# Hybrid diffusion trunk: RMSNorm by token-major statistics, with squares taken tile by tile and the high parts first

## The reference

```python
def _rmsnorm(x, g):
    xf = x.astype(jnp.float32)
    y = xf * lax.rsqrt(jnp.mean(xf * xf, axis=-1, keepdims=True) + NORM_EPS)
    return (y * g.astype(jnp.float32)).astype(x.dtype)
...
        h = _rmsnorm(x, W["norms"][l, 0]) * (1 + sc1) + sh1
        x = x + 0.5 * g1 * _swiglu(h, W["ffn_w1"][l, 0], W["ffn_w3"][l, 0], W["ffn_w2"][l, 0])
        h = _rmsnorm(x, W["norms"][l, 1]) * (1 + sc2) + sh2
        ...
        x = x + g2 * m.astype(x.dtype)
        h = _rmsnorm(x, W["norms"][l, 2]) * (1 + sc3) + sh3
        x = x + 0.5 * g3 * _swiglu(h, W["ffn_w1"][l, 1], W["ffn_w3"][l, 1], W["ffn_w2"][l, 1])
    return _rmsnorm(x, W["final_norm"]), (ak, av, bs, ck, cv)
```

## Time and profile before

| | us |
|---|---|
| timed runs, median of 3 | 3680.97 (3680.93 to 3685.23) |
| profiled execution, its own time | 3675.11 |
| its span | 3673.3 |
| PE busy | 3193.1 (87%) |
| DVE busy | 1676.1 (46%) |
| ACT busy | 981.8 (27%) |

### The profile page before, as it was taken

How to read it: one execution, slowest core, us unless ns; L and a number is a source line. 1 busy time by engine, 2 the same in 40 slices (tenths; PEclk the granted TensorE clock), 3 DMA queues, 4 the chain that set the end, 5 groups by cost and what they waited for, 6 DMA issues and landing times.

```text
span 3673.3 us, 61594 instructions
## 1 busy us (share of the span) xinstructions
PE 3193.1 (87%) x26174; PEld 2984.0 (81%) x26174; DVE 1676.1 (46%) x2575; ACT 981.8 (27%) x1724; POOL 0.2 (0%) x4
## 2 busy tenths in 40 slices
PE   7799998987688878899998999998975555899998
PEld 7799998975576667899998999998952224899997
DVE  2554545544445543554545454544135554422323
ACT  1212123213333322212123212123234343222222
POOL 0000000000000000000000000000000000000000
PEclk6899999986678888999999999999977667999999
DMA  6243433200000002244433444442200002222221
GB/s 213 69 120 109 124 111 92 75 14 0 16 5 4 5 4 75 83 113 120 126 95 100 109 121 116 113 121 62 69 8 6 4 6 60 58 69 80 70 79 52
DMA packets 393646, 264.16 MB, mean 72 GB/s; under 512 B 11627, under 2 KB 375430, under 8 KB 393350
## 3 DMA queue, kind: packets, MB, share of 16 engines
q1 hardware_dynamic: 393478, 261.71, 25.2%
HBM read 257.61 MB, written 4.06 MB: 71 GB/s over the span
## 4 chain that ended last, share of the span: by engine, by line
PE 82%; DVE 11%; ACT 3%; issue 2%; DMA 1%; SPq 0%; DVEq 0%; ACTq 0%
PE pair L2386 62%; PE pair L2372 2%; PE pair L1699 1%; PE pair L2352 1%; PE pair L2395 1%; DVE big L2206 1%; PE pair L829 1%; PE pair L812 1%; PE pair L1694 1%; PE pair L421 1%; DVE w_lo_as_f L1808 1%; PE pair L396 1%; DVE work L2200 1%; PE pair L1685 1%; PE pair L823 1%
## 5 line engine op out<-in xcount | busy, mean ns | idle before, releaser
L2386 PE MATMUL pair<-h_hi,w_hi 128*128 128x320 f32 x3792 | 874.7, 312 | 114.5 <-DVE h_lo L2215 68.1
L2386 PE MATMUL pair<-h_lo,w_hi 128*128 128x320 f32 x3792 | 872.6, 312 | 0.0
L2386 PE MATMUL pair<-h_hi,w_lo 128*128 128x320 f32 x3792 | 871.0, 311 | 0.0
L2386 PEld LDWEIGHTS pair<-h_hi,w_hi 128*128 128x128 f32 x3792 | 641.3, 190 | 118.3 <-issue 118.3
L2386 PEld LDWEIGHTS pair<-h_lo,w_hi 128*128 128x128 f32 x3792 | 642.3, 190 | 0.0
L2386 PEld LDWEIGHTS pair<-h_hi,w_lo 128*128 128x128 f32 x3792 | 641.7, 190 | 0.0
L2386 PE MATMUL pair<-big_as_f32r,w_hi 128*128 128x320 f32 x2816 | 540.6, 315 | 4.5 <-DVE w_lo L2105 4.5
L1995 ACT ACTIVATE w_hi<-raw 128x1024 fp32r<-128x1024 f32 x333 | 341.3, 1051 | 637.6 <-PE pair L2386 336.4
L2105 DVE TENSOR_TENSOR w_lo<-raw,w_hi 128x1024 fp32r<-128x1024 f32 x333 | 398.0, 1217 | 167.4 <-ACT w_hi L1995 166.7
L2386 PEld LDWEIGHTS pair<-big_as_f32r,w_hi 128*128 128x128 f32 x2816 | 453.5, 193 | 5.3 <-DVE w_lo L2105 5.3
L2250 DVE TENSOR_TENSOR work<-work,pair 128x640 f32<-128x640 f32 x88 | 72.3, 821 | 639.4 <-PE pair L2386 639.4
(11 more groups left out here) (346 smaller groups left out, 2868.0 us busy)
## 6 DMA issues: line engine op xcount, KB each, us to landing
raw<-ffn_w SPq DMA_DIRECT2D x272, 512.0 KB, 5.1
work<-mod_w SPq DMA_DIRECT2D x136, 512.0 KB, 3.8
raw<-w_in_c SPq DMA_DIRECT2D x24, 512.0 KB, 3.7
raw<-w_in_ab SPq DMA_DIRECT2D x21, 512.0 KB, 4.0
w_hi_as_f<-mod_w SPq DMA_DIRECT2D x8, 512.0 KB, 4.6
raw<-w_out_ab SPq DMA_DIRECT2D x8, 512.0 KB, 5.7
raw<-w_out_c SPq DMA_DIRECT2D x8, 512.0 KB, 5.1
h_hi_as_f<-x_sample SPq DMA_DIRECT2D x1, 2048.0 KB
```

The source lines that it names most:

```text
L2386: ins = nc.tensor.matmul(ps[:, c, 0:HALF], w, v[:, k, c * HALF:(c + 1) * HALF], start=(k == 0 and w is hi and v is xh), stop=(k == kts - 1 ...
```

## The change

For norms 1 to 6 the squares no longer stand in the norm. In the stage ahead of it ACT squares tile j right after DVE has updated it, into two small buffers in turn (the first tile straight into the sum), and DVE adds the tiles 1 to 6 into `sq_acc`; the last square stays apart. Norm 0 still squares its eight tiles first.

The mean is formed with tokens on the partitions: the squares are the weights, 64 tokens at a time, and one column of 1/1024 is the moving operand, so 20 calls of one column for two parts (80 for norm 0's eight). Root and reciprocal work on `rt5`, 128 tokens by 5, and five matmuls spread it over the partitions into the pair that DVE then reads while scaling. That pair is `norm_pair(k)`, `pp[(norm_at[k] + 2) % 4]`, no longer the one of the next stage's first slab. ACT's load of the root's table is put at the start of the stage ahead.

After a norm PE takes the first two slabs together (`two_slabs`): all products with `h_hi` of both, tile by tile as `n_hi` comes, then those with `h_lo`.

```diff
+        sq_acc = work[:, 5376:6016]
+        sq_t = (work[:, 4096:4736], work[:, 4736:5376])
+        rt5 = work[:, 6016:6021]
...
+        def norm_pair(k):
+            return pp[(norm_at[k] + 2) % 4]
...
-                for t in range(DT):
-                    if k:
-                        act.wait_ge(pair_free, norm_at[k] + RING - DT + t + 1)
-                    nc.scalar.activation(norm_t[:, t, :], x[:, t, :], ACT.Square).then_inc(n_sq, 1)
+                if k == 0:
+                    for t in range(DT):
+                        nc.scalar.activation(norm_t[:, t, :], x[:, t, :], ACT.Square).then_inc(n_sq, 1)
                 act.wait_ge(n_sum, k + 1)
-                nc.scalar.activation(halves(rt_t), pp[norm_at[k] % 4][:, :, 0:HALF], ACT.Sqrt, bias=eps[:, 0:1]).then_inc(n_root, 1)
+                nc.scalar.activation(rt5, norm_pair(k)[:, 0, 0:NCH], ACT.Sqrt, bias=eps[:, 0:1]).then_inc(n_root, 1)
...
                 elif kind in ("down", "out"):
+                    if before_norm(i):
+                        nc.scalar.preload_act_table(ACT.Sqrt)
                     for j in range(cnt):
                         if j + 2 < cnt or ahead:
                             split_hi(0, n0 + j + 2)
+                        if before_norm(i):
+                            act.wait_ge(pair_free, n0 + j + 1 + RING)
+                            if j > 2:
+                                act.wait_ge(n_acc, (DT - 2) * (norm_after(i) - 1) + j - 2)
+                            nc.scalar.activation(sq_t[j % 2] if j else sq_acc, x[:, j, :], ACT.Square).then_inc(n_sq, 1)
...
-                nc.vector.reciprocal(rt_t, rt_t).then_inc(n_recip, 1)
-                dve.wait_ge(n_recip, k + 1)
+                nc.vector.reciprocal(rt5, rt5).then_inc(n_recip, 1)
+                dve.wait_ge(n_spread, k + 1)
...
-                                                             in1=rt_t[:, a:b], op0=ALU.mult, op1=ALU.mult)
+                                                             in1=norm_pair(k)[:, g, 0:b - a], op0=ALU.mult, op1=ALU.mult)
...
+                        if before_norm(i) and j >= 2:
+                            k = norm_after(i)
+                            dve.wait_ge(n_sq, DT * k + j)
+                            if j > 2:
+                                dve.wait_ge(n_acc, (DT - 2) * (k - 1) + j - 2)
+                            nc.vector.tensor_tensor(sq_acc, sq_acc, sq_t[(j - 1) % 2], ALU.add).then_inc(n_acc, 1)
...
-                pair = pp[norm_at[k] % 4]
+                pair = norm_pair(k)
                 if k == 0:
                     pe.wait_ge(m_taken, COLUMNWISE * DT // 4 + 2)
+                    pe.wait_ge(mod_fin, 2)
+                    parts = [norm_t[:, t, :] for t in range(DT)]
                 else:
-                    pe.wait_ge(pair_free, norm_at[k] + 1)
-                for t in range(DT):
-                    pe.wait_ge(n_sq, DT * k + t + 1)
-                    for c in range(2):
-                        ins = nc.tensor.matmul(pair[:, c, 0:HALF], mean_d, norm_t[:, t, c * HALF:(c + 1) * HALF],
-                                               start=(t == 0), stop=(t == DT - 1))
+                    pe.wait_ge(pair_free, norm_at[k] + 3)
+                    pe.wait_ge(n_acc, (DT - 2) * k)
+                    parts = [sq_acc, sq_t[(DT - 1) % 2]]
+                for t, part in enumerate(parts):
+                    if k == 0 or t:
+                        pe.wait_ge(n_sq, DT * k + (t + 1 if k == 0 else DT))
+                    for j in range(NCH):
+                        for h in range(2):
+                            ins = nc.tensor.matmul(pair[h * HD:(h + 1) * HD, 0, j:j + 1],
+                                                   part[:, j * P + h * HD:j * P + (h + 1) * HD], mean_d[:, 0:1],
+                                                   start=(t == 0 and j == 0), stop=(t == len(parts) - 1), skip_group_check=True)
                 ins.then_inc(n_sum, 1)
+                pe.wait_ge(n_recip, k + 1)
+                for j in range(NCH):
+                    ins = nc.tensor.matmul(pair[:, j // 4, j % 4 * P:(j % 4 + 1) * P], rt5[:, j:j + 1].to_broadcast([P, P]), ident,
+                                           start=True, stop=True)
+                ins.then_inc(n_spread, 1)
...
+            def two_slabs(n0, kk):
+
+                for j in (n0, n0 + 1):
+                    pe.wait_ge(lo_full, j + 1 + RING)
+                    pe.wait_ge(pair_free, j + 1)
+                for k in range(DT):
+                    pe.wait_ge(n_hi, DT * kk + k + 1)
+                    for j in (n0, n0 + 1):
+                        for w in (w_hi, w_lo):
+                            for c in range(2):
+                                nc.tensor.matmul(pp[j % 4][:, c, 0:HALF], w[:, j % RING, k, :], h_hi[:, k, c * HALF:(c + 1) * HALF],
+                                                 start=(k == 0 and w is w_hi), stop=False)
+                for j in (n0, n0 + 1):
+                    for k in range(DT):
+                        if j == n0:
+                            pe.wait_ge(n_lo, DT * kk + k + 1)
+                        for c in range(2):
+                            ins = nc.tensor.matmul(pp[j % 4][:, c, 0:HALF], w_hi[:, j % RING, k, :], h_lo[:, k, c * HALF:(c + 1) * HALF],
+                                                   start=False, stop=(k == DT - 1))
+                    ins.then_inc(slab_used, 1)
...
+                    if key in norm_before:
+                        two_slabs(n0, norm_before[key])
+                        slab(0, n0 + 2, kts, k0, xh, xl, None)
+                        slab(0, n0 + 3, kts, k0, xh, xl, None)
```

More of the change, by code:

```diff
@@ L178, in build @@
         prod_t = work[:, 4736:5376].rearrange("p (a b) -> p a b", a=2)
-        rt_t = work[:, 5376:6016]
+        sq_acc = work[:, 5376:6016]
+        sq_t = (work[:, 4096:4736], work[:, 4736:5376])
+        rt5 = work[:, 6016:6021]
         def col(i, n=1):
@@ L220, in build @@
         n_sq, n_sum, n_root, n_recip, n_scaled, n_hi, n_lo = NM
+        n_acc, n_spread = sem("norm_acc"), sem("norm_spread")
         stages = []
@@ L265, in halves2, with before_norm, norm_after @@
             return ap[:, t, :].rearrange("p (a b) -> p a b", a=2)
+        def before_norm(i):
+            return i + 1 == len(stages) or stages[i + 1][:4] in norm_before
+        def norm_after(i):
+            return NORMS - 1 if i + 1 == len(stages) else norm_before[stages[i + 1][:4]]
+        def norm_pair(k):
+            return pp[(norm_at[k] + 2) % 4]
         def LOOKAHEAD(i):
@@ L2420, in stage @@
                     looped = cnt // 4 * 4
-                    with pe.Fori(0, cnt // 4) as i2:
+                    if key in norm_before:
+                        two_slabs(n0, norm_before[key])
+                        slab(0, n0 + 2, kts, k0, xh, xl, None)
+                        slab(0, n0 + 3, kts, k0, xh, xl, None)
+                    with pe.Fori(1 if key in norm_before else 0, cnt // 4) as i2:
                         for j in range(4):
-                            slab(i2, n0 + j, kts, k0, xh, xl, tile_ready if j == 0 else None)
+                            slab(i2, n0 + j, kts, k0, xh, xl, tile_ready if j == 0 and key not in norm_before else None)
                 else:
```

## The result

The changed kernel takes 3595.92 us (median of 4 runs, 3593.77 to 3598.24), the kernel before in the same session 3683.10 (4 runs, 3680.93 to 3689.00): a ratio of 0.9766, 95% interval 0.9748 to 0.9783. The forecast was 3610, the range 3594 to 3637. The profiled execution took 3596.85 us, its span is 3595.1, which is 78.2 under the span before.

The account below looks back on a forecast made before the run. PE bounds the kernel, idling long at the norms. 5 x 12.9 + 6.4 + 1.8 - 1.4 = 71.3 us off 3675.1 gives 3603.8; with 5.9 for the median, 3610. Range 3594 to 3637 with the first rival.

Parts of the forecast that it names:

- Statistics, norms 1 to 5: Mean calls after the last slab, 40 records: taken as 2.4 us, from the half-clock RWKV row with 64x64 weights.
- The lower bound: For the 40 records of the mean calls: about 1.4 us, from a full-clock row of 40 records in 0.79.
- Norm 0: First norm: 160 records at the half clock, 9.6 us against 10.91; PE starts 1.8 us earlier.
- The first rival: Short mean calls run at the upper bound's pace: +2.5 us at six norms, +10 at norm 0, 3635; 20%.
- Root, reciprocal, spread: On 128x5 root, reciprocal and hand-over 0.5 us, spread 2.4; scaling starts at E+7.45, E being PE's leaving the last slab.
- Restart: After a norm PE starts on the first h_hi at E+9.45 instead of E+22.39, 12.9 us earlier at five norms.
- Does PE run dry?: In the two slabs after a norm, PE waits at most 0.3 us between high and low parts.
- Third slab: After the two slabs, its low weights wait on DVE: 0.7 us charged at norms 2 and 3, 1.4 in all.
- Added waits: In stages ahead of a norm, squares make ACT wait for updates before splitting: 4.2 us against 10.6, costed at nothing.
- The third rival: ACT's squares make weights late in the six stages ahead of a norm: 3812, at half of that about 3710; 3%.
- Second rival: The clock does not come back in the two slabs: about 10 us more at five norms, 3660; 4%.
- From the profiled execution to the median: From 3603.8 to 3610, since the timed median before lay 5.9 us above the profiled execution.

Follow-up runs that it names:

- experiment 1: The changed kernel with the new statistics but without the high parts first, PE taking slabs one by one after a norm: 3626.92 us, ratio 0.9850.
- experiment 3: The changed kernel with one statistics call of 128 weight columns instead of two halves of 64, half as many calls: 3618.93 us, ratio 0.9836.
- experiment 7: The changed kernel with 13 idle matmuls of 128x320 before the statistics and again behind the spread: 3590.83 us, ratio 0.9761.
- experiments 9 to 11: One session, in order: the changed kernel, it with norm 0 early, that with idle matmuls added too: 3598.85, 3584.25, 3578.99 us.

## Why the prediction came out as it did

The mechanism was right at every norm; the gain in the profiled execution was forecast as 71.3 and is 78.2. By steps:

- **Squares and sums:** ready at E+2.15 by the prediction; the calls start at E+2.21. Right.
- **Statistics, norms 1 to 5:** the term that was mis-sized. "I take 2.4, the row nearest in weight columns and in pairing, for all norms"; measured 1.33. The row of 2.4 was taken at the half clock, but here the calls follow a dense slab: in the windows of the changed kernel the clock is full over the calls of norm 1, and of norms 2 to 5 too, which all took 1.33, and at norm 1 it falls only after them (first the calls, then the spread):

```profile
609.72:611.05 1.33, 1.33 (x40) 1.24 (x40) 0.00 (x0) 0.00 (x0) 0.00 (x0) 1.00 0.13 37
611.63:614.13 2.50, 2.50 (x10) 2.21 (x10) 0.00 (x0) 0.00 (x0) 0.00 (x0) 0.50 0.00 0
```

  The lower bound, from the row at the full clock, was the right one; with the measured 1.33 it is worth 1.07 at each of five norms, 5.4 us. The bound's own working does not give its 1.4: ten groups in 0.79 make 1.6 for twenty, so that 1.4 came so near is in part luck. At the final norm the clock fell during the calls, which took 2.06. The place alone does not fix the clock either: in experiment 1 the same calls at norm 1 had 0.50 and took 2.30.
- **Norm 0:** 160 records in 8.70, at 0.50 throughout, for a forecast of 9.6; restart 2.6 us earlier for 1.8. Per 40 records that is 2.18 with weights of 128 rows, where the row with 64 rows had 2.40 at the same clock. That row also has 64 moving columns, and its pairs lie in different row halves as well, so it is experiment 3 that tells: with 128 rows in both, half as many calls of twice the columns took nearly twice as long. The Trainium skill, "TensorE: Matmul & The Clock Gate", section "LDWEIGHTS (loading the stationary operand)", has the rule that a load costs by its columns and not by its rows; the trace agrees that rows do not add. The first rival, with 4.9 at a norm and 19.6 here, falls by the measured 1.33 and 8.70.
- **Root, reciprocal, spread:** hand-overs and two small steps 0.58 for 0.5, the spread 2.50 for 2.4. At norms 2, 3 and 4 the clock stayed up into the spread, and the scaling starts at E+6.48, 5.88 and 6.12 where the others have 6.66; the forecast of E+7.45 less the 1.07 above leaves 6.38.
- **PSUM as operand:** no difference, 7.42 for 7.49. Right.
- **Restart:** 2.20 after the scaling for 2.0. In all 13.5 to 14.3 us earlier at each of the five norms, 69.1 for the forecast 64.5.
- **Does PE run dry?** No wait between high and low parts, for "at most 0.3". The half clock lasted 3.3 to 5.9 us after the restart, the forecast's 3.0 to 5.7; what PE loses there is why it does not get ahead of DVE: in experiment 7, without the half clock, it waits in the low parts at norm 1.
- **Third slab:** 0.7 charged at two norms, none seen: no gap stands there. 1.4 us too much.
- **Added waits:** nothing, right; the last feed-forward took 467.22 for 467.07, the six stages between the norms 3408.7 for 3407.3 in sum. The third rival, slower than before, falls.
- **Second rival:** the clock came back within the two slabs at every norm. It falls.
- **From the profiled execution to the median:** I added 5.9 since before's median lay above its profiled execution. That was no property of the kernel: the runs of before lie between 3662 and 3698 in all sessions together, and after's own median is 0.9 below its profiled execution. This step costs 6.8, as much as all errors of the sum together.

So 4.6 (restarts), 0.1 (final norm), 0.8 (norm 0) and 1.4 (third slab) make the 6.9 by which the sum was too small, and the median adds 6.8; but for rounding that is the distance from 3610 to 3596. Both errors point the same way, so the time lies inside the range by only 2 us.

## What to carry to other kernels

A row's duration on PE belongs to the clock it was granted: before a row is borrowed, look at what PE does just ahead of the new place, and take the row at that level, with the other level as the bound. Where an early start is bought, follow the chain of the producer to its last piece (here DVE's 14.9 us of scaling and low parts): it bounds what a quicker consumer can still gain. Sum the gaps of the bound engine over both traces first; when they give the whole difference, what single stages gain and lose cancels, and none of it has to be explained by the change.

## What the runs showed of the hardware that was not expected

One-column matmuls can keep PE busy and still be followed by the half clock, and the dense work behind them pays. In the kernel with norm 0 early, PE at the end of the first down stage, and the window behind it:

```profile
216.08 0.75 PE L2434 MATMUL pair<-big_as_f32r,w_hi 128*128 128x320 f32 x4
216.67 0.46 PE L2434 MATMUL pair<-big_as_f32r,w_lo 128*128 128x320 f32 x2
216.96 4.58 PE L2443 MATMUL pair<-eps,big 128*128 128x1 f32 x32
221.40 1.41 PE L2434 MATMUL pair<-big_as_f32r,w_hi 128*128 128x320 f32 x4
```
```profile
218.00:227.00 9.00, 9.00 (x47) 9.00 (x47) 7.46 (x10) 1.06 (x1) 0.00 (x0) 0.62 0.60 174
```

The same four matmuls of a slab take 1.41 us behind these calls and 0.75 ahead of them, with no idle time between. There are 15 such groups of 32 in each kernel; in the trace of the changed kernel the clock fell within or right behind 11 of them. In the first feed-forward there are five: the clock fell at two in the first trace of experiments 9 to 11 (and once behind a wait of 2.1 us), at all five in the second. What decides at which groups it falls, stays open. But it is what makes equal stages differ: the first feed-forward lasts 490.7 to 498.9 us in the thirteen traces, and 482.8 to 484.4 in all of them when half of its time at the half clock is taken off.
